# Gate and up products of a SwiGLU layer with the activations stationary, and the product turned on TensorE

## The reference, cut to what matters

```
def swiglu(h, w_gate, w_up, w_down):
    return (jax.nn.silu(h @ w_gate) * (h @ w_up)) @ w_down
```

## Time and profile before

| what | value |
|---|---|
| time, median of 3 runs | 3128.18 us (3126.63 to 3132.62) |
| the profiled execution: time | 3126.05 us |
| the profiled execution: span | 3124.4 us |
| mean granted TensorE clock | 0.911 |
| TensorE matmuls, busy | 2705.2 us (87%) |
| VectorE busy | 2088.8 us (67%) |
| ScalarE busy | 1110.8 us (36%) |
| bytes moved | 615.40 MB, mean 197 GB/s |

### The profile page before, as it was taken

How to read it: one execution, slowest core, us unless ns; L and a number is a source line. 1 busy time by engine, 2 the same in 40 slices (tenths; PEclk the granted TensorE clock), 3 DMA queues, 4 the chain that set the end, 5 groups by cost and what they waited for, 6 DMA issues and landing times.

```text
span 3124.4 us, 52445 instructions
## 1 busy us (share of the span) xinstructions
PE 2705.2 (87%) x20804; PEld 2623.4 (84%) x20804; DVE 2088.8 (67%) x2381; ACT 1110.8 (36%) x1073; POOL 478.2 (15%) x614
## 2 busy tenths in 40 slices
PE   1388887466679799999999979999879999999997
PEld 1387777455579699999999969999869999999997
DVE  6879998566757576776767658746757654445454
ACT  0234444322213433333333343344343433333333
POOL 1059995111110000000000001100000000000000
PEclk6599999655569899999999989999989999999998
DMA  9753233223348378787787739944637755555551
GB/s 341 252 192 108 97 104 108 73 91 105 108 150 277 116 267 280 270 275 272 264 283 264 266 109 323 324 145 155 221 127 262 273 193 189 187 181 196 178 186 68
DMA packets 287568, 615.40 MB, mean 197 GB/s; under 512 B 22220, under 2 KB 22755, under 8 KB 286947
## 3 DMA queue, kind: packets, MB, share of 16 engines
q1 hardware_dynamic: 252642, 479.64, 45.4%
q0 software_dynamic: 34816, 134.23, 12.1%
HBM read 611.73 MB, written 2.10 MB: 196 GB/s over the span
## 4 chain that ended last, share of the span: by engine, by line
PE 68%; issue 13%; DVE 10%; POOL 4%; ACT 4%; DMA 1%; SPq 0%; DVEq 0%; POOLq 0%; ACTq 0%
PE groups L1481 21%; PE groups L1483 21%; PE groups L1485 21%; DVE w_lo L1146 2%; PE pm L1460 1%; PE pb L1514 1%; PE pa L1509 1%; ACT act_hi L995 1%; ACT w_hi L946 1%; POOL dn_mb L614 1%; DVE ada_acc L1323 1%; ACT xT L1020 1%; DMA ada_units<-in_ada_w_dram 1%; DVE s_z L1372 1%; DVE s_z L1379 1%
## 5 line engine op out<-in xcount | busy, mean ns | idle before, releaser
L1481 PE MATMUL groups<-act_hi,w_hi 128*128 128x256 f32 x4800 | 1382.8, 288 | 104.6 <-DVE w_lo L1146 55.0
L1146 DVE TENSOR_TENSOR w_lo<-w_raw,w_hi 128x2048 fp32r<-128x2048 f32 x388 | 894.2, 2306 | 715.1 <-ACT w_hi L946 713.4
L1483 PE MATMUL groups<-act_lo,w_hi 128*128 128x256 f32 x4800 | 1369.9, 285 | 0.0
L1485 PE MATMUL groups<-act_hi,w_lo 128*128 128x256 f32 x4800 | 1369.0, 285 | 0.0
L946 ACT ACTIVATE w_hi<-w_raw 128x2048 fp32r<-128x2048 f32 x386 | 738.2, 1913 | 1229.7 <-PE groups L1485 1229.2
L1481 PEld LDWEIGHTS groups<-act_hi,w_hi 128*128 128x128 f32 x4800 | 933.9, 195 | 120.6 <-DVE w_lo L1146 63.1
L1483 PEld LDWEIGHTS groups<-act_lo,w_hi 128*128 128x128 f32 x4800 | 934.3, 195 | 0.2
L1485 PEld LDWEIGHTS groups<-act_hi,w_lo 128*128 128x128 f32 x4800 | 933.2, 194 | 0.0
L1136 DVE SCALAR_TENSOR_TENSOR ada_acc<-ada_units,c_act,ada_acc 128x512 f32<-128x512 f32 x600 | 467.3, 779 | 23.4 <-DMA ada_units<-in_ada_w_dram 6.2
L1481 PE MATMUL groups<-hid_hi,w_hi 128*128 128x256 f32 x1408 | 390.7, 277 | 0.0
L1483 PE MATMUL groups<-hid_lo,w_hi 128*128 128x256 f32 x1408 | 389.9, 277 | 0.0
(11 more groups left out here) (323 smaller groups left out, 2173.8 us busy)
## 6 DMA issues: line engine op xcount, KB each, us to landing
ada_units<-in_ada_w_dram POOLq DMA_DIRECT2D x128, 1024.0 KB, 6.3
w_raw<-in_ffn_w_gate_dram SPq DMA_DIRECT2D x88, 1024.0 KB, 5.1
w_raw<-in_ffn_w_up_dram SPq DMA_DIRECT2D x88, 1024.0 KB, 5.1
w_raw<-in_ffn_w_down_dram SPq DMA_DIRECT2D x88, 1024.0 KB, 5.1
w_raw<-in_cd_w_in_dram SPq DMA_DIRECT2D x48, 1024.0 KB, 5.8
ada_units<-in_ada_w_dram SPq DMA_DIRECT2D x40, 1024.0 KB, 5.0
w_raw<-in_ab_w_in_dram SPq DMA_DIRECT2D x40, 1024.0 KB, 5.0
ada_first<-in_ada_w_dram SPq DMA_DIRECT2D x24, 1024.0 KB, 9.9
```

Of the source, the lines that this page charges most:

```text
L1146: dve.tensor_tensor(wlo[:, half], raw[:, slot], whi[:, half].bitcast(F32), ALU.subtract).then_inc(lo_done, 1)
L1481: pe.matmul(dst, whi[:, j % 2, kk, cols], hi[:, k], start=(q == 0 and kk == 0 and n % 2 == 0), stop=False, skip_group_check=True)
L1483: pe.matmul(dst, whi[:, j % 2, kk, cols], lo[:, k], start=False, stop=False, skip_group_check=True)
L1485: last = pe.matmul(dst, wlo[:, j % 2, kk, cols], hi[:, k], start=False, stop=(q == p["units"] - 1 and kk == UK - 1), skip_group_check=True)
```

## The change

In the gate and up products the two operands change places. The stationary operand becomes a 128 x 128 piece of the activations (128 tokens of one feature tile, high or low part), and the moving operand 512 columns of the weights, high or low part. A unit is 4 k-tiles x 2 token halves x 3 = 24 matmuls, and its result has tokens on the partitions: `pgf[:, 2 * (g % 2) + b]` holds 128 tokens x 512 columns. tanh and the two multiplications read the same PSUM tensor in that layout and are written as before.

The down product still needs features on the partitions, so TensorE turns `gate_s` with 8 transposes of 128 x 128 per group (`hid_turn`), four into the PSUM tensor `pa` and four into `pb`. ScalarE copies each bank to `hhi` (`hid_high`), VectorE subtracts for `hlo` (`hid_low`), both from PSUM in pieces of 128 x 512. The three steps of a group stand behind the first unit of the next body, or, for the last group of a block, behind the first unit of the down product. `hid_turned` is new, `hid_hi` and `hid_lo` now count two per group, and `hid_lo` starts at 2. For this the first body of these loops is written out, and the rest run as a loop (`first=True`). The products other than gate and up keep their matmuls.

```diff
@@ bodies, the same for every engine
-        def bodies(engine, n, body, peel=False):
+        def bodies(engine, n, body, peel=False, first=False):
             if n == 1:
                 body(0)
+            elif first:
+                body(0)
+                with engine.Fori(0, n - 1) as i:
+                    body(i + 1)
@@ ScalarE, ffn
                         else:
-
-                            act.wait_ge(grp_done, p["g0"] + 2 * i + 2 + 2)
-                            act.activation(hhi[:, bass.ds(GT * i, GT)], gs[:], ACT.Copy).then_inc(hid_hi, 1)
-                    product(p, up)
+
+                    def turned(i, j, done=FFN_GROUPS * layer + first - 1):
+                        if j == 0 and not (isinstance(i, int) and i == 0):
+                            hid_high(done + i, GT * (i - 1))
+                    product(p, up, after=turned, first=True)
                     p = by_name[f"down{layer}{n}"]
-                    product(p, None)
+
+                    def last_turned(i, j, done=FFN_GROUPS * layer + first + groups - 1, at=GT * (groups - 1)):
+                        if isinstance(i, int) and i == 0 and j == 0:
+                            hid_high(done, at)
+                    product(p, None, after=last_turned, first=True)
+
+            def hid_high(group, at):
+
+                for c, bank in enumerate((pa, pb)):
+                    act.wait_ge(hid_turned, 2 * group + c + 1)
+                    k = slice(at + 2 * c, at + 2 * c + 2) if isinstance(at, int) else bass.ds(at + 2 * c, 2)
+                    act.activation(hhi[:, k], bank[:].rearrange("p (a l) -> p a l", a=2), ACT.Copy).then_inc(hid_hi, 1)
@@ VectorE
+            def hid_low(group, at):
+
+                for c, bank in enumerate((pa, pb)):
+                    dve.wait_ge(hid_hi, 2 * group + c + 1)
+                    k = slice(at + 2 * c, at + 2 * c + 2) if isinstance(at, int) else bass.ds(at + 2 * c, 2)
+                    dve.tensor_tensor(hlo[:, k], bank[:].rearrange("p (a l) -> p a l", a=2), hhi[:, k].bitcast(F32),
+                                      ALU.subtract).then_inc(hid_lo, 1)
...
                             dve.scalar_tensor_tensor(gs[:], gs[:], 0.5, pg[:, 1], ALU.mult, ALU.mult).then_inc(grp_done, 1)
-                            dve.wait_ge(hid_hi, done + i + 1)
-                            dve.tensor_tensor(hlo[:, bass.ds(GT * i, GT)], gs[:],
-                                              hhi[:, bass.ds(GT * i, GT)].bitcast(F32), ALU.subtract).then_inc(hid_lo, 1)
@@ TensorE, product
-                            for n in range(GT):
+                            for b in range(2 if wide else 0):
+                                dst, rows = pgf[:, 2 * (g % 2) + b], slice(P * b, P * b + P)
+                                pe.matmul(dst, hi[:, k, rows], whi[:, j % 2, kk], start=(k == 0), stop=False,
+                                          skip_group_check=True)
+                                pe.matmul(dst, lo[:, k, rows], whi[:, j % 2, kk], start=False, stop=False,
+                                          skip_group_check=True)
+                                last = pe.matmul(dst, hi[:, k, rows], wlo[:, j % 2, kk], start=False,
+                                                 stop=(k == UK * p["units"] - 1), skip_group_check=True)
+                            for n in range(0 if wide else GT):
@@ TensorE, ffn
-                    product(by_name[f"up{layer}{n}"], on_act(2 * layer + 1))
-                    product(by_name[f"down{layer}{n}"],
-                            lambda q, done=FFN_GROUPS * layer + first: pe.wait_ge(hid_lo, done + q + 1), hhi, hlo)
+                    up, down = by_name[f"up{layer}{n}"], by_name[f"down{layer}{n}"]
+
+                    def turned(i, j, done=FFN_GROUPS * layer + first - 1, g0=up["g0"]):
+                        if j == 0 and not (isinstance(i, int) and i == 0):
+                            pe.wait_ge(grp_done, g0 + 2 * i + 2)
+                            hid_turn(done + i)
+
+                    def last_turned(i, j, done=FFN_GROUPS * layer + first + groups - 1, g0=up["g0"] + 2 * groups):
+                        if isinstance(i, int) and i == 0 and j == 0:
+                            pe.wait_ge(grp_done, g0 + 2)
+                            hid_turn(done)
+                    product(up, on_act(2 * layer + 1), after=turned, wide=True, first=True)
+                    product(down, lambda q, done=FFN_GROUPS * layer + first: pe.wait_ge(hid_lo, 2 * (done + q + 1) + 2),
+                            hhi, hlo, after=last_turned, first=True)
+
+            def hid_turn(group):
+
+                hid = gs[:].rearrange("p a l -> p (a l)").rearrange("p (b n) -> p b n", b=2)
+                for c, bank in enumerate((pa, pb)):
+                    pe.wait_ge(hid_lo, 2 * group + c + 1)
+                    for f in range(2):
+                        for b in range(2):
+                            last = pe.transpose(bank[:, L * f + P * b:L * f + P * b + P],
+                                                hid[:, b, P * (2 * c + f):P * (2 * c + f) + P], ident[:])
+                    last.then_inc(hid_turned, 1)
```

More of the change, by code:

```diff
@@ L208, in build @@
         grp_done = sem("grp_done")
-        gate_t, hid_hi, hid_lo = sem("gate_t"), sem("hid_hi"), sem("hid_lo")
+        gate_t, hid_hi, hid_lo, hid_turned = sem("gate_t"), sem("hid_hi"), sem("hid_lo"), sem("hid_turned")
         ada_step = sem("ada_step")
@@ L946, in split_hi, with product @@
                 act.activation(whi[:, j % 2], raw[:, (j + 2) % 4], ACT.Copy).then_inc(hi_done, 1)
-            def product(p, evacuate, before=None, after=None):
+            def product(p, evacuate, before=None, after=None, first=False):
                 def body(i):
@@ L964, in body @@
                             after(i, j)
-                bodies(act, p["bodies"], body, peel=before is not None)
+                bodies(act, p["bodies"], body, peel=before is not None, first=first)
             def take(dst):
@@ L1147, in split_lo, with product @@
                                   ALU.subtract).then_inc(lo_done, 1)
-            def product(p, evacuate, before=None, after=None, lag=0, skip_last=False):
+            def product(p, evacuate, before=None, after=None, lag=0, skip_last=False, first=False):
                 def body(i):
@@ L1169, in body @@
                             after(i, j)
-                bodies(dve, p["bodies"], body, peel=before is not None)
+                bodies(dve, p["bodies"], body, peel=before is not None, first=first)
+            def hid_low(group, at):
[4 more added lines that the diff above has]
+                                      ALU.subtract).then_inc(hid_lo, 1)
             def ffn(layer):
@@ L1184, in up, with turned, last_turned @@
                             dve.scalar_tensor_tensor(gs[:], gs[:], 0.5, pg[:, 1], ALU.mult, ALU.mult).then_inc(grp_done, 1)
-                            dve.wait_ge(hid_hi, done + i + 1)
-                            dve.tensor_tensor(hlo[:, bass.ds(GT * i, GT)], gs[:],
-                                              hhi[:, bass.ds(GT * i, GT)].bitcast(F32), ALU.subtract).then_inc(hid_lo, 1)
-                    product(p, up)
+                    def turned(i, j, done=FFN_GROUPS * layer + first - 1):
+                        if j == 0 and not (isinstance(i, int) and i == 0):
+                            hid_low(done + i, GT * (i - 1))
+                    def last_turned(i, j, done=FFN_GROUPS * layer + first + groups - 1, at=GT * (groups - 1)):
+                        if isinstance(i, int) and i == 0 and j == 0:
+                            hid_low(done, at)
+                    product(p, up, after=turned, first=True)
                     p = by_name[f"down{layer}{n}"]
@@ L1193, in ffn @@
                         dve.wait_ge(ln_gb, 4 * (2 * layer + 1))
-                    product(p, into_x)
+                    product(p, into_x, after=last_turned, first=True)
             def into_x(i, g, units):
@@ L1257, in _ @@
             dve.sem_inc(grp_done, 2)
+            dve.sem_inc(hid_lo, 2)
             dve.sem_inc(ada_step, ADA_FREE)
@@ L1461, in ada_sum, with product @@
                 last.then_inc(ada_summed, 1)
-            def product(p, ready, hi=None, lo=None, mid=None, after=None):
+            def product(p, ready, hi=None, lo=None, mid=None, after=None, wide=False, first=False):
                 hi, lo = hi if hi is not None else ahi, lo if lo is not None else alo
@@ L1492, in body @@
                             after(i, j)
-                bodies(pe, p["bodies"], body, peel=after is not None)
+                bodies(pe, p["bodies"], body, peel=after is not None, first=first)
             def on_act(n):
```

3 lines of the change are left out of this document (2 added, 1 removed).

## The result

| | median | lowest to highest |
|---|---|---|
| before | 3130.4 us (4 runs) | 3126.63 to 3133.18 |
| after | 3097.15 us (4 runs) | 3094.61 to 3098.7 |

The ratio is 0.9892, with a 95% interval of 0.9879 to 0.9905: faster by 33 us, where 76 were forecast. The time lies at the upper end of the range, 1 us from what rival (a) gave, 3096.

What follows compares the result with a forecast made beforehand. TensorE's issue rate was taken to bound both feed-forward layers. Shorter steps 98.6, less transposes 19.1 and waits 3.3, gave 76.2 us off the profiled 3126.05, so 3049.9; forecast 3051 us, 8-in-10 range 3040 to 3098.

Steps and rivals of the forecast that it cites:

- rival (a): Gate/up matmuls: overhead paid per matmul, 512-column step 0.227 us, gain 32 us, 3096 us; 14% with the cases between.
- the choice of the step's length: Gate/up 512-column matmuls: step taken as 0.216 us, 0.576 us less per unit, 98.6 us over 171.3 units.
- the layer-norm sums: TensorE's layer-norm matmuls, 256 columns at two cycles: step 0.216 us, load hidden; taken as model for the new step.
- The argument from the ada sums: One-column ada matmuls step by 0.10 us, read as the weight load's floor, which a 0.107 us stream can't hide.
- The transposes' term: Eight added TensorE transposes per feed-forward group: 0.87 us a group, 19.1 us over 22 groups.
- the waits': TensorE waiting for gate_s before transposes in seven groups without ada work: five of 0.54, two of 0.28, 3.3 us.
- Rival (c): Feed-forward transposes cost 0.28 us each: 30 us more, 3081 us; chance 5%.
- rival (f): VectorE late in ada bodies by 1 us a body: 15 us, 3066 us; counted with the forecast's 68%.
- the tight case: Ada bodies: VectorE's ada unit plus w_lo take 5.39 us against a 5.18 us unit, slack shrinking to 0.2 us.
- Rival (b): Gate/up: a 512-column float32r matmul costs two of 256, step 0.240 us, some 3147 us; 8% in the final chances.
- Rival (d): Feed-forward: waits and transposes let TensorE's granted clock fall, 22 stretches costing 41 us, 3092 us; chance 4%.
- Rival (e): Gate/up step far under 0.213 us, TensorE outrunning the splits: 213 us off, some 2915 us; chance 1%.

## Why the prediction was wrong

**The step that failed** is the choice of the step's length: "I take 0.216: 24 x 0.216 = 5.18 us, 0.576 us less per unit." Measured are 0.2267 us and 5.44 us, 0.32 us less per unit. The reason given was that the layer-norm sums are "the nearest row, since both its stream and its load are of the same length". They are of the same length, and yet it is the wrong neighbour: their stream is float32 at two cycles per column, and the float32 run pays 1 to 3 ns at that pace on these very tiles, where float32r pays 13 and bfloat16 12. The argument from the ada sums, that a stream of 0.107 us "can just not hide" the load, would have the 13 ns vanish at 0.213 us; they did not: 384 columns step by 0.17 to 0.18 us for 0.160 and 512 by 0.2267 for 0.213, and half a load did not shorten the step. And with the hidden tiles moved onto a multiple of 128 bytes the 0.114 us of the earlier trace rows became 0.120 with the load unchanged. The neighbour to take was the float32r row of the same code, 0.120 us: its columns plus 0.013, paid per matmul, which is the bound 0.227 that the prediction had worked out and left to rival (a).

That 3097 us still lies within 3040 to 3098 is no merit of the forecast's mechanism: the range had been stretched to the end of rival (a), which had a chance of 14% together with the cases between.

**The sum with what was measured.** 171.3 units x 0.32 us = 54.8 us won. 22 groups x 0.90 us = 19.8 us for the transposes. Waits: a body without ada work took 2724.13 - 2679.37 = 44.76 us, that is 8 x 5.44 and 1.24 more, 0.34 over the transposes; five of these make 1.7 us, and before the two down stages TensorE did not wait. Net 33.3 us; the medians differ by 33.3. The transposes' term stands, and the waits' is as sized for units of 5.44 us, but for the two down stages.

**Point by point.**
- TensorE sets the pace before and after: held. It is busy in 717.00 of 717.00 and in 705.33 of 706.00 us.
- 0.87 us a group for the transposes, taken from the S5 stage: 0.90, and the run with two transposes confirms 0.11 us for each that was taken away. Rival (c), 0.28 each, is refuted: it took the length for the step. The Trainium skill's 275 ns ("TensorE: Matmul & The Clock Gate", section "Part 4: PE-mode transpose"), given there for bfloat16, is the length here too, with float32 (0.27 us). The step in place is 0.11.
- Waits only in bodies without ada work, for `gate_s`: held in five groups; 0.28 us for a unit of 5.44 us had been worked out, and the transposes come 0.26 us late (0.32 in two of the five). Before the two down stages, where 0.28 us was forecast, they start 0.12 us after the matmul before them, as in the down stages with ada work: no wait.
- VectorE in time in ada bodies, rival (f): not late. Units of 5.44 us are also slower than the forecast's 5.18, so the tight case was not put to the test.
- Weights in time: held; the transfer share is 0.80 at 275 GB/s. `hid_hi` twice 0.58 us and `hid_lo` twice 0.68: as sized.
- Rival (b), 0.240 us: refuted, and the run cut at 256 columns shows what it would have cost (3160.64 us, one run, where 3147 was worked out: its feed-forwards took 20.5 us more than those of before, close to the 19.1 of the forecast's transposes, and the rest lies in stages outside them, 8 us of it ahead of the first feed-forward). Rival (d), the clock: 1.00 in every window of both layers. Rival (e): no step under 0.213 us.
- The Trainium skill's rule for the gap, N/2.4 + 2.5 ns ("TensorE: Matmul & The Clock Gate", section "Back-to-back issue gap"): with float32, counted at two cycles per column, the trace agrees at both lengths with a few ns over the columns (0.216 and 0.428 us). With float32r the rule gives 215.8 ns where 226.7 were measured, and 109.2 where 113 to 120 were.

**What stays open.** That the 13 ns are paid per matmul and depend on the place of the act and hidden tiles, as the moving and as the stationary operand, is shown; that they are nearly absent with plain float32 too. What in the chip takes them is not: neither the load's length nor the operands' exchange does. Nor is it shown what moves a step from 113 to 117 ns on unchanged places, or why a gap of 96 bytes gives nothing in the mean. No place of the weight tiles was tried, so whether a tile's own place counts or its place against the weights' is open.

## What to carry to other kernels

When a trace lacks an operation, take first the row that shares its format and its pace, not the one that happens to last as long; write its time as columns plus a constant and keep the constant. Where TensorE is the bound, fewer and longer matmuls win that constant once for each matmul saved, here 24 x 13.3 ns per unit, and the transposes that the new layout asks for took a third of it back. Before exchanging operands, move a tile by 32 or 64 bytes, check in the built program where it and the tiles behind it begin, and read the step again: it cost two lines and gave 18 us (64 bytes) to 30 us (32 bytes, one run), where the whole change gave 33.

## What the runs showed of the hardware

- A float32r matmul of 256 columns at clock 1.00 stepped by 0.120 us with its moving operand at a multiple of 128 bytes. When only the places of tiles were moved, by 32, 64 or 192 bytes, the mean was 0.116 to 0.117 us and single steps began at 0.113. At 512 columns the mean steps were 227.6, 229.7 and 233.9 ns with the stationary operand moved by 0, 192 and 32 bytes.
- The best place was not the same in the two layouts: act tiles moved by 32, 64 or 192 bytes were better as the moving operand of 256 columns (116.0 to 117.4 ns for 119.9) and, by 32 or 192, worse as the stationary one beside 512 columns (229.7 and 233.9 ns for 227.6, mean steps).
- Plain float32, at two cycles per column (0.428 us for 512), showed 1 to 3 ns over its columns in the same places; bfloat16, read in steps of two elements, 12 ns (0.225 us).
- A matmul of 128 columns stepped by 0.11 us, twice its columns. Cutting each 512 into 384 and 128 made the kernel 249 us slower than after (one run).
- A 128x128 float32 transpose between matmuls cost 0.11 us, though it lasts 0.27 us.
- Loading 64 columns for 128 made the 512-column step longer, 0.230 us for 0.227.
